# The first input projection of a two-block transformer: modulation by feature rows, sixteen output blocks summed at once in eight banks by full fp32 products, eighteen as whole wide blocks

## The reference

```python
c_act = jax.nn.silu(c)                         # c: (1, 2048)
mod = c_act @ w_ada[l] + b_ada[l]              # (1, 6 * 2048)
sh_a, sc_a, gt_a, sh_f, sc_f, gt_f = split(mod, 6)
h = _rmsnorm(x, norm_mix[l]) * (1.0 + sc_a) + sh_a
p = h @ w_in[l]                                # (256, 9296)
c_q, c_kv, k_pe, q_g, k_g, v_g, z, b_logit, a_logit, gate_logits = _split_cols(p)
```

## Time and profile before

| | us |
|---|---|
| median of 3 runs | 2864.57 |
| lowest to highest | 2861.81 to 2866.37 |
| span of the profiled execution, first to last instruction | 2856.0 |
| TensorE busy in that span | 2747.0 (96%) |
| VectorE busy | 2033.0 (71%) |
| ScalarE busy | 1360.4 (48%) |
| GpSimd busy | 208.1 (7%) |

### The profile page before, as it was taken

How to read it: one execution, slowest core, us unless ns; L and a number is a source line. 1 busy time by engine, 2 the same in 40 slices (tenths; PEclk the granted TensorE clock), 3 DMA queues, 4 the chain that set the end, 5 groups by cost and what they waited for, 6 DMA issues and landing times.

```text
span 2856.0 us, 43985 instructions
## 1 busy us (share of the span) xinstructions
PE 2747.0 (96%) x17404; PEld 2439.8 (85%) x17404; DVE 2033.0 (71%) x2983; ACT 1360.4 (48%) x2169; POOL 208.1 (7%) x180
## 2 busy tenths in 40 slices
PE   6988999999999999999999999999999999999997
PEld 6888778888889888888888889998788888888886
DVE  7898786777797886555556688996567566575665
ACT  3445653343444544444444554465654444444454
POOL 0231000000002000000000080111110000000001
PEclk9999999999999999999999999999999999999999
DMA  9864255656787686555555555554445555555553
GB/s 392 314 228 134 95 172 186 198 192 206 236 304 268 217 305 226 191 188 188 191 185 192 187 169 169 177 165 139 153 130 182 190 187 191 187 190 189 188 190 127
DMA packets 158461, 565.31 MB, mean 198 GB/s; under 512 B 17584, under 2 KB 21936, under 8 KB 158256
## 3 DMA queue, kind: packets, MB, share of 16 engines
q1 hardware_dynamic: 158256, 562.50, 58.9%
HBM read 560.33 MB, written 2.10 MB: 197 GB/s over the span
## 4 chain that ended last, share of the span: by engine, by line
PE 85%; DVE 9%; ACT 3%; issue 2%; DMA 1%; SPq 0%; POOL 0%; DVEq 0%; ACTq 0%; POOLq 0%
PE BK L350 20%; PE BK L348 19%; PE BK L351 10%; PE BK L347 10%; PE BK L353 6%; PE BK L355 5%; PE BK L354 5%; DVE LO L657 2%; PE BK L435 2%; ACT HI L517 1%; DVE ADA L653 1%; DVE B L865 1%; DVE B L707 1%; PE BK L360 1%; PE BK L461 1%
## 5 line engine op out<-in xcount | busy, mean ns | idle before, releaser
L517 ACT ACTIVATE HI<-RAW 128x1024 fp32r<-128x1024 f32 x825 | 875.1, 1061 | 1253.7 <-PE BK L348 862.3
L657 DVE TENSOR_TENSOR LO<-RAW,HI 128x1024 fp32r<-128x1024 f32 x825 | 1017.9, 1234 | 376.2 <-ACT HI L517 373.0
L350 PE MATMUL BK<-H,HI 128*128 128x512 f32 x2528 | 1009.5, 401 | 9.0 <-DVE LO L657 8.5
L348 PE MATMUL BK<-H,HI 128*128 128x512 f32 x2496 | 985.3, 396 | 0.0
L351 PE MATMUL BK<-H,LO 128*128 128x256 f32 x2528 | 703.0, 278 | 0.0
L347 PE MATMUL BK<-H,LO 128*128 128x256 f32 x2496 | 698.2, 280 | 0.4 <-DVE H L703 0.2
L353 PE MATMUL BK<-H,HI 128*128 128x256 f32 x1840 | 545.6, 296 | 33.6 <-DVE B L707 15.7
L347 PEld LDWEIGHTS BK<-H,LO 128*128 128x128 f32 x2496 | 469.7, 188 | 111.8 <-DVE H L703 2.0
L351 PEld LDWEIGHTS BK<-H,LO 128*128 128x128 f32 x2528 | 477.0, 189 | 99.7 <-issue 1.0
L354 PE MATMUL BK<-H,HI 128*128 128x256 f32 x1840 | 523.8, 285 | 0.0
L355 PE MATMUL BK<-H,LO 128*128 128x256 f32 x1840 | 523.6, 285 | 0.0
(11 more groups left out here) (244 smaller groups left out, 1870.5 us busy)
## 6 DMA issues: line engine op xcount, KB each, us to landing
RAW<-wst_dram SPq DMA_DIRECT2D x825, 512.0 KB, 3.9
RAW<-wada_dram SPq DMA_DIRECT2D x155, 512.0 KB, 4.5
EARLY<-wada_dram SPq DMA_DIRECT2D x37, 512.0 KB, 7.8
EARLY<-wst_dram SPq DMA_DIRECT2D x33, 512.0 KB, 6.7
X<-xT_dram SPq DMA_DIRECT2D x8, 512.0 KB, 8.8
B<-bias_dram SPq DMA_DIRECT2D x32, 128.0 KB, 3.4
out_dram<-X SPq DMA_DIRECT2D x3, 512.0 KB, 2.7
CN<-consts_dram SPq DMA_DIRECT2D x1, 840.0 KB, 8.1
```

The lines of the kernel that those rows point to most:

```text
L348: e.matmul(bk[:, :], hh, H[:, k, :], start=False, stop=last, skip_group_check=True).then_inc(S["tile"], 1)
L350: e.matmul(bk[:, :], hh, H[:, k, :], start=first, stop=False, skip_group_check=True)
L517: e.activation(HI[:, u % NHL, :], raw_at(slot), ACT.Copy).then_inc(S["hi"], 1)
L657: e.tensor_tensor(LO[:, u % NHL, :], raw_at(slot), HI[:, u % NHL, :].bitcast(f32), sub).then_inc(S["lo"], 1)
```

## The change

**Modulation.** The 64 "A" units are laid out anew on the host: a unit now has 128 output features on the partitions and 1024 of the 2048 inputs along the row, so that four units (shift and scale, two halves each) give shift and scale of one input block. The silu of `c` is spread to all partitions: 16 products of 128 columns (`c_spread`) and four copies (`c_row`). Per unit VectorE multiplies in place (`unit_product`) and ScalarE copies with an accumulated sum (`unit_sum`). Three small operations (`mod_row`) make scale and shift, `x_scaled` applies the norm, and `modulated` makes the block `HF[j]` in plain fp32. `split` still fills `H1`, now from `HF`.

**First projection.** `FIRST`, 16 of the 34 blocks, is summed row by row of input blocks in all eight banks, two blocks a bank: `direct` multiplies the landed fp32 tile by `HF[k]`, with no `hi` and no `lo`. A row needs 4 "R" and 2 "D" units. Rows are modulated two ahead. `REST`, 18 blocks, then runs as whole wide blocks. `partial`, `ev_part`, the GpSimd additions and the `LATE` pass are gone. The input `x` is loaded ahead of the weights. The `tanh` of the convolution starts right behind the last row.

```diff
-ERA = 17
+ROWS_AHEAD = 2
+DIRECT = 16
...
+            def direct(slot, i, bk, o, k, last, raw, h, free):
+                q.wait_ge(raw, h, free)
+                e.matmul(bk[:, o:o + 256], raw_at(slot)[:, 128 * i:128 * i + 128], HF[k], start=(k == 0 and o == 0), stop=last,
+                         skip_group_check=True).then_inc(S["tile"], 1)
+
+            def c_spread(bk, i, c, consts, free):
+                q.wait_ge(c, consts, free)
+                for n in range(4):
+                    r = e.matmul(bk[:, 128 * n:128 * n + 128], SC[:, 4 * i + n:4 * i + n + 1].broadcast_to([128, 128]), cn("ident"), start=True, stop=True)
...
+            def unit_sum(slot, c, product):
+                q.wait_ge(product)
+                e.activation(raw_at(slot), raw_at(slot), ACT.Copy, accum_out=SM[:, c:c + 1]).then_inc(S["ada_a"], 1)
+
+            def modulated(j, mod, x):
+                q.wait_ge(mod, x)
+                e.activation(HF[j], X[:, j, :], ACT.Identity, bias=MOD[:, j:j + 1], scale=SC[:, 32 + j:33 + j]).then_inc(S["ev_a"], 1)
...
+            def unit_product(slot, half, raw, row):
+                q.wait_ge(raw, row)
+                e.tensor_tensor(raw_at(slot), raw_at(slot), CR[:, 1024 * half:1024 * half + 1024], mult).then_inc(S["ada"], 1)
...
-            kinds = ["A"] * 16
-            for g in range(GROUPS - 1):
...
+            kinds = ["R"] * (4 * ROWS_AHEAD)
+            for i in range(16):
+                kinds += ["D"] * (DIRECT // 8) + ["R"] * (4 if i + ROWS_AHEAD < 16 else 0)
...
+            def row_unit(j, i):
+                s, slot = st["proc"], slot_of(st["proc"])
+                v = do("unit_product", "ada", slot, i % 2, raw(s), cr_tok)
+                raw_free[slot] = do("unit_sum", "ada_a", slot, 4 * j + i, v)
...
+                for f in list(row_done):
+                    next(f, None)
+                if i == 3:
+                    row_done.append(row_end(j, raw_free[slot]))
+
+            def row_end(j, sums):
+                x = do("x_scaled", "ad_v", j, rs_tok[0], tk_x[j // 4])
+                m = do("mod_row", "mod_v", j, sums, tk_cols, n=3)
+                yield
+                hf_tok[j] = do("modulated", "ev_a", j, m, x)
+                yield
+                h_tok[j] = yield from split(H1, j, HF[j], hf_tok[j])
...
-            for k in range(0, 12, 4):
-                partial(range(k, k + 4))
...
+            for r in range(16):
+                if r + ROWS_AHEAD < 16 + 1 and r > 0:
+                    for i in range(4):
+                        row_unit(r + 1, i)
+                while hf_tok[r] is None:
+                    next(row_done[0], None)
+                direct_row(r)
...
-            for n in Q03:
-                run(block(H1, h_tok, 0, "w_in", 0, n, ev_qkv(n - 9), LATE))
             later(qkv_chain(), 0, TAPS)
-            for n in Q47:
-                run(block(H1, h_tok, 0, "w_in", 0, n, ev_qkv(n - 9), LATE))
+            for n in REST:
+                run(block(H1, h_tok, 0, "w_in", 0, n, ev_qkv(n - 9, True), wide=True))
```

More of the change, by code:

```diff
@@ L289, in program @@
         GB = [GBT[:, i, :] for i in range(16)]
[L290 removed]
+        ACC = ADA[:, :]
         PIF = 3.1415925
@@ L1236, in partial, with __init__, release @@
-            def partial(ks):
-                for c, n in enumerate(CBLK + Q03 + Q47):
-                    first = ks[0] == 0
-                    if first:
-                        part_tok[n] = None
-                    run(block(H1, h_tok, 0, "w_in", 0, n, ev_part(n, first, c % 2 == 1), ks))
-            for k in range(0, 12, 4):
-                partial(range(k, k + 4))
-            need(h_tok, 15)
-            def half_of(n):
-                return part[n], need(part_tok, n)
+            class Halves:
+                def __init__(self, ring, i):
+                    self.ring, self.i, self.used = ring, i, []
+                def release(self, half, *signals):
+                    self.used.append(list(signals))
+                    if len(self.used) == 2:
+                        self.ring.release(self.i, *self.used)
@@ new lines, in walk, with direct_row @@
+            held = []
+            for b in range(DIRECT // 2):
+                ring = lbank if lbank.idle else mbank
+                bi, bk, fr = ring.get()
+                held.append((Halves(ring, bi), bk, fr))
+            hi_tok.update({u: None for u in range(2 * DIRECT)})
+            done_tok = [None] * DIRECT
+            def direct_row(r):
+                for g in range(DIRECT // 8):
+                    s = lin_at[w.tile // 8]
+                    slot = slot_of(s)
+                    for i in range(8):
+                        b = 8 * g + i
+                        own, bk, fr = held[b // 2]
+                        w.tile += 1
+                        if log is not None:
+                            log.append(("w_in", r, FIRST[b]))
+                        done_tok[b] = do("direct", "tile", slot, i, bk, 256 * (b % 2), r, r == 15, raw(s), need(hf_tok, r), fr if r == 0 else None)
+                    raw_free[slot] = done_tok[b]
+                    assert st["proc"] == s
+                    st["proc"] += 1
+                    while load_next():
+                        pass
+                    w.flush()
@@ new lines, in walk @@
+            for r in range(16):
+                if r + ROWS_AHEAD < 16 + 1 and r > 0:
+                    for i in range(4):
+                        row_unit(r + 1, i)
+                while hf_tok[r] is None:
+                    next(row_done[0], None)
+                direct_row(r)
+            while row_done:
+                next(row_done[0], None)
+            r_last = ("ada", w.count["ada"])
+            p1_end = [("tile", w.tile), h_tok[15], r_last]
+            feed(w.tile // 8 + 1)
@@ L1297, in ev_kpe @@
             def ev_kpe(bk, tok, own):
-                half, hk = half_of(8)
-                k = combine(KPE, bk, half, add, tok, own, hk)
+                k = copy_out(KPE, bk, tok, own)
                 yield
@@ L1306, in walk, with ev_qkv @@
             raw_tok = [None] * 24
-            def ev_qkv(j):
+            def ev_qkv(j, wide):
                 def f(bk, tok, own):
-                    half, hk = half_of(9 + j)
-                    raw_tok[j] = combine(B1[:, j, :], bk, half, add, tok, own, hk)
-                    yield
+                    if wide:
+                        raw_tok[j] = yield from raw_sum(B1[:, j, :], bk, tok, own, x_stat)
+                    else:
+                        raw_tok[j] = copy_out(B1[:, j, :], bk, tok, own, x_stat)
+                        yield
                 return f
@@ L1333, in ev_ba @@
             def ev_ba(bk, tok, own):
-                half, hk = half_of(41)
-                lin_tok["ba"] = combine(BA, bk, half, add, tok, own, hk, tk_cos)
+                lin_tok["ba"] = copy_out(BA, bk, tok, own, tk_cos)
                 yield
```

168 lines of the change are left out of this document (76 added, 92 removed).

## The result

The changed kernel takes 2880.11 us (median of 4 runs, 2877.82 to 2881.75), the kernel before 2863.19 (2861.72 to 2866.37, 4 runs). The ratio is 1.0062, with a 95% interval of 1.0049 to 1.0074: it is slower, beyond the 0.2% that can be told from no change. The forecast was 2850.5 us, and the range ended at 2874.

The account below looks back on a forecast made before the run. First projection held by waits, transfers to about 80 us, then VectorE; TensorE behind it. Direct stage 141 plus REST 142 leaves the projection's end at 283; -14 behind it, from 2864.6, gives 2850.5 us, range 2818 to 2874.

Parts of the forecast that it names:

- The start: Ahead of the first row: modulated block ready for the first direct product at 25 us, cold TensorE losing 1.7 us.
- The row stage: Direct products of 16 rows, first projection: ends at 141 us, with transfers and TensorE close and other engines hidden.
- the last unit lands at 135.8, and TensorE needs 8 x 0.445 more: End of the direct stage reckoned by bytes at 409 GB/s: 139.4 us.
- Row cost by engine: Direct stage, per row: transfers 7.7 us, TensorE 7.1, VectorE 6.5, ScalarE 5.9.
- Rival C: Direct stage: rows take 8.7 instead of 7.1 us as VectorE waits for ScalarE; 25 us slower, 2875.5; chance 0.2.
- `REST`: Remaining 18 blocks of the first projection: 142 us, between ends of 107 and 165, projection ending at 283 us.
- `l2norm`: Within REST: two table loads, root and eight scalings add about 7 us on VectorE.
- 65 + 68 + 7: REST's terms: unit 12's residue near 65 us, 12 blocks of link and two units 68 us, l2norm about 7.
- a load adds no drain: ScalarE table loads in REST: the skill's 1.38 us drain, up to 17 us for twelve loads, counted as none.
- Behind the projection: All after the projection: -7 from l2norm, -6 from the chain, -1 from an earlier delta rule; sum -14 us.
- `l2norm`'s -7: Attention stage: l2norm products for four heads have moved out of it, -7 us.
- The -6 for attention without the chain: Attention stage: with one or two links left instead of 18, TensorE loses time at the next stretch's rate, -6 us.

Follow-up runs that it names:

- later angles: Changed kernel with the 16 waiting steps ahead of the rotary angles put back: 2868.94 us, ratio to before 1.0028.
- `l2norm` behind and the chain in front: Changed kernel with angles later and the first l2norm queued behind the 288 tiles of REST: 2861.49 us, ratio to before 1.0001.
- whole chain behind: Changed kernel with angles later, whole convolution chain and first l2norm queued behind the projection: 2841.57 us, ratio to before 0.9930.
- chain behind the norms: Changed kernel with angles later, convolution chain starting only after the second latent normalisation and the scalars: 2852.89 us, ratio to before 0.9976.
- links overlapped and spread: Chain behind the norms with links overlapped, l2norm behind REST, a link per 12 tiles: 2840.95 us, 0.9924; with row's closing steps first 2834.34 us, 0.9908.
- constants earlier: Changed kernel with positions and second constants loaded behind the 14th weight load instead of the 40th: 2871.10 us, ratio to before 1.0035.

## Why the prediction was wrong

**The start** was near: the first direct product stands at 26.8 us instead of 25, and row 1 at 36.4 instead of 33.8, since row 0 took 9.6 us on a lower clock where 8.8 were counted. It costs nothing, since from row 6 on landings pace the rows anyway once the gap is closed.

**The row stage** (141, was 160.6) is the step that failed. Of the 19.6 us, 12.7 are the wait of `angle`. The prediction listed what VectorE does in a row as four products, a scaling, three small steps and a residue, and took the row's cost from that list. It went through what the change adds, not through what else now stood in VectorE's order between the rows: L713 with its wait for constants and positions. The other 6.9 are a term that was mis-sized: "the last unit lands at 135.8, and TensorE needs 8 x 0.445 more". With later angles the last unit landed at 137.7, and TensorE was done at 147.9: it had two rows of work from the landing at 133.9 on, 14 us. Row cost by engine was right: 6.91 us of TensorE where transfers don't bound, 7.67 where they do, VectorE hidden, busy 5.3 to 6.5 us a row (27.70 of 40 us and 29.01 of 34). Rival C (8.7 us a row, VectorE waiting for ScalarE in every row) didn't happen, though its time of 2875.5 is near the result. The right sign for the wrong reason: VectorE's order did decide, in one place of 16 us, not in sixteen places.

The limit of about 358 GB/s that the Trainium skill gives (DMA: Bandwidth & Descriptors, Specifications) would have ended the stage at 158 us. The stage did end at 160.6, but not by that: with later angles the transfers run at 409 and 410 GB/s from 60 to 134 us. The trace disagrees with that limit here, where one core runs the program, and that the sums agree was chance.

**`REST`** (142, was 153.9). Its first half came out as worked out from order and rows: residues of its fifth, sixth, seventh and twelfth unit end at 28.4, 38.4, 44.0 and 66.0 us for 28.5, 38.5, 44 and 65. TensorE's idle time ahead of the fifth and sixth was 7.7 and 7.5 us for 10 and 7. The mis-sized term is `l2norm`. Of the 11.9 us, 5.8 are its own: 12.8 measured against 7, because to its operations comes the wait for the rounding that stands ahead of them on ScalarE. Another 4.6 are the difference between two executions with the same order in `REST`, and the clock told below explains them. 1.5 us are left over. (The recorded terms, 65 + 68 + 7, make 140 and not 142, so the 1.5 are 3.5 against their sum.) That table loads are a large part of it was right, and that a load adds no drain as well: eleven loads stand between 168 and 197 us, where the schedule by 1.28 us each holds to 0.5 us up to the seventh unit.

**Behind the projection** (-14, was -9.5). `l2norm`'s -7 was right: 6.6. The -6 for attention without the chain, worked out from the busy shares of two stretches, was mis-sized. With `l2norm` behind and the chain in front, TensorE stands like this in the two stretches of the same length:

```profile
285.00:366.00 81.00, 78.92 (x520) 63.80 (x519) 45.03 (x100) 47.66 (x124) 0.00 (x0) 1.00 0.29 99
366.00:452.00 86.00, 82.14 (x504) 66.25 (x503) 60.08 (x86) 36.03 (x68) 0.00 (x0) 1.00 0.53 173
```

The first did gain what the term says, 78.92 against 74.20 of 81 us. But the next lost part of it, 82.14 against 84.77 of 86. Over both it is 161.1 us with no more than one link, 159.0 with 18 (before) and 156.5 with 24 (whole chain behind: 76.96, then 79.56 of 86). So 18 links cost about 2 us here and not 6: the term took it for granted that the next stretch keeps its rate. This too is rough, since the granted clock was 0.96 in one stretch of either of the latter. Spans can't tell such sizes. This part takes 2574.3, 2573.4 and 2578.9 us in these three kernels, and the 2573.4 are of the short execution. An estimate that goes by medians (median less the profiled end of the projection) gives 2576.7, 2578.0 and 2582.9, in the order that the term needs. By it the part behind is 15 us shorter after the change and 6 us with later angles, where the order is the same, so this estimate is good to some 5 us at best, and how far short of -14 the part fell stays open.

In sum: predicted -14 of 2856.0; 12.7 the wait, 6.9 the tail of the row stage, 11.9 `REST`, 4.5 behind, 0.4 the end of before. The steps that failed are the wait of `angle`, which the prediction put at nothing, and the end of the row stage, `l2norm` and the chain's cost in attention, which it mis-sized. With the first two edits that follow from this (angles later, chain behind the norms) the change is worth 0.24% instead of costing 0.6%, and with the links overlapped and spread as well 0.9%.

## What to carry to other kernels

When a diff moves a load or takes out waiting steps, find in the new order every instruction that waits for that load, and ask what stands behind it on its engine: here one early consumer in VectorE's order stopped TensorE for 16 us, and the transfers with it. When a stage is bound by transfers, its end is not the last byte plus a little: find the first landing from which on the work that lands takes longer than the landings, and count all the work from there. Steps that use different function tables belong apart in the order, and idle time in a stretch may be put down to some work only when a run without that work shows it.

## What the hardware showed that I had not expected

The profiled executions of the changed kernel and of the one with later angles have the same order in `REST`, and the same short idle time of TensorE in `l2norm` (7.88 of 10 us busy, with one pause of 1.87 us). Behind it the granted clock fell in the one and not in the other. After the change, from 260 us:

```profile
260.00:270.00 10.00, 7.88 (x25) 5.45 (x24) 8.61 (x16) 4.03 (x8) 0.00 (x0) 0.71 0.32 107
270.00:280.00 10.00, 10.00 (x39) 7.20 (x38) 3.43 (x7) 2.44 (x4) 0.00 (x0) 0.78 0.31 105
```

With later angles, from 247 us:

```profile
247.00:257.00 10.00, 7.88 (x39) 5.67 (x38) 8.60 (x17) 5.18 (x9) 0.00 (x0) 1.00 0.32 107
257.00:267.00 10.00, 10.00 (x53) 7.88 (x52) 7.97 (x16) 3.52 (x6) 0.00 (x0) 1.00 0.40 130
```

A mean of 0.71 is a mixture of 2.4 GHz and 1.2 GHz (the level of 0.50 that 60 to 74 us show). From the residue of `REST`'s 17th unit to that of the 24th it is 30.1 us in both. From there to the 29th, behind the pause, it is 21.0 us in one and 16.3 in the other. The kernel with constants earlier lies between: the same pause, a clock of 0.69 and 0.63 in the two 5 us stretches from 251 us on, and 19.2 us. So the same pause cost 4.7 us, 2.9 us or nothing. The last two ran on the same chip, so it isn't the chip. What decides it these runs don't show.
